# Refilling an expert weight ring in smaller fetches, copying gathered tokens earlier, and turning the activation in two halves

## What is computed

```python
def expert_block(args):
    xb, e = args
    hdn = xb @ w_up[e] + b_up[e]              # 1024 -> 2048
    x_glu = jnp.minimum(hdn[:, :D_FF], SWIGLU_LIMIT)
    x_lin = jnp.clip(hdn[:, D_FF:], -SWIGLU_LIMIT, SWIGLU_LIMIT)
    act = x_glu * jax.nn.sigmoid(SWIGLU_ALPHA * x_glu) * (x_lin + 1.0)
    return act @ w_down[e] + b_down[e]        # 1024 -> 1024
...
h = h + merged @ w_out[l]
h = h + moe_ffn(rms_norm(h, norm_ffn_g[l]), w_router[l], b_router[l], w_up[l], b_up[l], w_down[l], b_down[l])
h = rms_norm(h, norm_final_g)
```

## Time and profile before

| | us |
|---|---|
| median of 3 runs | 1189.77 |
| the profiled execution | 1189.58 |
| its span, first to last instruction | 1187.70 |
| PE busy | 1142.3 (96%) |
| mean granted TensorE clock, share of full speed | 0.997 |
| up of expert 0 starts at | 284.84 |
| up of expert 2 starts at | 344.17 |
| up of expert 4 starts at | 399.71 |

### The profile page before, as it was taken

How to read it: one execution, slowest core, us unless ns; L and a number is a source line. 1 busy time by engine, 2 the same in 40 slices (tenths; PEclk the granted TensorE clock), 3 DMA queues, 4 the chain that set the end, 5 groups by cost and what they waited for, 6 DMA issues and landing times.

```text
span 1187.7 us, 13231 instructions
## 1 busy us (share of the span) xinstructions
PE 1142.3 (96%) x5598; PEld 529.4 (45%) x5598; DVE 229.6 (19%) x527; ACT 187.3 (16%) x376; POOL 0.2 (0%) x4
## 2 busy tenths in 40 slices
PE   9999999999999999999999999999999999999996
PEld 7767888844243333333333334343333333333332
DVE  4555620114111111111111111111211111111112
ACT  2257620012010111101010101010110101000103
POOL 0000000000000000000000000000000000000000
PEclk9999999999999999999999999999999999999999
DMA  9834434384999999999999999999999999999996
GB/s 376 342 145 178 149 118 162 144 350 177 411 427 429 434 426 435 430 434 429 436 428 435 429 431 433 430 433 430 435 429 436 428 435 429 433 431 430 427 428 263
DMA packets 25117, 441.97 MB, mean 372 GB/s; under 512 B 4033, under 2 KB 4545, under 8 KB 7297
## 3 DMA queue, kind: packets, MB, share of 16 engines
q1 hardware_dynamic: 22464, 439.19, 87.5%
q10 hardware_dynamic: 2624, 2.39, 0.6%
HBM read 440.52 MB, written 1.05 MB: 372 GB/s over the span
## 4 chain that ended last, share of the span: by engine, by line
PE 83%; DMA 13%; ACT 2%; issue 1%; DVE 1%; ACTq 0%; SPq 0%; another core or an unknown queue 0%
PE ps L867 32%; PE ps L886 16%; DMA work<-in_w_exp_dram 12%; PE ps L525 11%; PE ps L842 4%; PE ps L854 4%; PE ps L734 2%; PE ps L797 2%; PE ps L817 2%; ACT work L1277 1%; PE ps L876 1%; PE ps L758 1%; PE ps L602 1%; DVE work L1720 1%; DMA ring<-in_w_mix_dram 1%
## 5 line engine op out<-in xcount | busy, mean ns | idle before, releaser
L867 PE MATMUL ps<-ring,work 128*64 128x512 f32 x1536 | 341.7, 597 | 5.6 <-DMA ring<-in_w_exp_dram 3.7
L867 PEld LDWEIGHTS ps<-ring,work 128*64 128x64 f32 x1536 | 108.5, 137 | 222.9 <-issue 216.6
L1719 DVE TENSOR_SCALAR work<-ps 128x512 f32<-128x512 f32 x32 | 22.1, 691 | 718.5 <-PE ps L867 718.5
L525 PE MATMUL ps<-work,ring 128*128 128x256 f32 (+2 forms) x576 | 129.6, 384 | 0.0
L886 PE MATMUL ps<-work 128*64 128x512 f32 x512 | 113.8, 595 | 10.6 <-ACT work L1277 10.3
L886 PE MATMUL ps<-ring,work 128*64 128x512 f32 x512 | 113.6, 595 | 8.4 <-ACT work L1277 7.0
L867 PE MATMUL ps<-work 128*64 128x512 f32 x512 | 116.0, 596 | 0.5 <-DMA work<-in_w_exp_dram 0.5
L525 PEld LDWEIGHTS ps<-work,ring 128*128 128x128 f32 (+1 forms) x576 | 107.1, 188 | 19.1 <-issue 1.2
L854 PE MATMUL ps<-work 64*128 64x512 f32 x256 | 71.7, 639 | 0.0
L886 PEld LDWEIGHTS ps<-work 128*64 128x64 f32 x512 | 35.2, 137 | 79.2 <-issue 62.8
L886 PEld LDWEIGHTS ps<-ring,work 128*64 128x64 f32 x512 | 35.5, 137 | 76.3 <-issue 65.1
(11 more groups left out here) (234 smaller groups left out, 620.8 us busy)
## 6 DMA issues: line engine op xcount, KB each, us to landing
ring<-in_w_exp_dram SPq DMA_DIRECT2D x56, 4096.0 KB, 33.6
work<-in_w_exp_dram SPq DMA_DIRECT2D x28, 4096.0 KB, 32.9
ring<-in_w_exp_dram SPq DMA_DIRECT2D x16, 2048.0 KB, 24.8
ring<-in_w_mix_dram SPq DMA_DIRECT2D x29, 1024.0 KB, 7.3
work<-in_w_exp_dram SPq DMA_DIRECT2D x6, 2048.0 KB, 20.0
work<-in_w_exp_dram SPq DMA_DIRECT2D x4, 1024.0 KB, 43.3
ring<-in_w_mix_dram SPq DMA_DIRECT2D x2, 576.0 KB, 17.8
work<-in_x_dram SPq DMA_DIRECT2D x2, 512.0 KB, 17.8
```

What stands on the lines that cost most here:

```text
L525: ins = nc.tensor.matmul(ps[part:part + width, b, 0:hi - lo], wv[:, k, o:o + width], xnT[:, k, lo:hi], start=(k == 0), stop=(k == KT - 1))
L867: ins = nc.tensor.matmul(ps[CAP * c:CAP * c + CAP, b, :], xeT[:, k, CAP * (u % 2):CAP * (u % 2) + CAP], wu[:, k % SPAN, 512 * q:512 * q + ...
L1719: V.tensor_scalar(hg, ps[:, 0, :], LIMIT, None, ALU.min).then_inc(glu_ready, 1)
```

## The change

There are four parts.

1. **Ring.** Experts 2 and 3 are fetched in units of 2 slots, and the very first unit in two halves of one slot each. `weights_used` now grows by one with every up step instead of by two with every second one. The loop over pairs starts with expert 4; the experts that no longer fill a group of four (28 and 29) are written out behind it.
2. **First copies.** ACT copies the first gather as soon as each half is done, ahead of the wait for `seed` and of its two DMAs.
3. **Turned activation.** `turn_act` puts the first two transposes into bank 3 and the other two into bank 2, each half with its own signal. ACT copies each half (256 columns) as it comes. `down` waits for the first half ahead of step 0 and for the second ahead of step 1. Since bank 2 also holds the turned routing weights, `turn_route` moves ahead of `up_bias`, both scatters are done first, and ACT copies the routing weights ahead of the activation.
4. **Root's table.** The dummy root that ACT runs to load the table of functions moves from ahead of the branch to behind it.

```diff
+            for h in range(SPAN):
+                spe.wait_ge(weights_used, M0 + h + 1)
+                spe.dma_start(RING[0][:, SLOT * h:SLOT * h + SLOT], w_exp[2, 0, :, SLOT * h:SLOT * h + SLOT])\
+                   .then_inc(unit_loaded[0], 16)
+            for n, c in [(2, c) for c in range(1, UNITS_E)] + [(3, c) for c in range(UNITS_E)]:
+                spe.wait_ge(weights_used, M0 + PER_EXPERT * (n - 2) + SPAN * (c + 1))
+                fetch(n, c)
...
-            with spe.Fori(0, (E - 4) // UNROLL) as it:
+            with spe.Fori(0, (E - 8) // UNROLL) as it:
                 for u in range(UNROLL):
                     for p in range(3):
-                        spe.wait_ge(weights_used, it * (UNROLL * PER_EXPERT) + (M0 + PER_EXPERT * u + 4 * (p + 1)))
...
+                        spe.wait_ge(weights_used, it * (UNROLL * PER_EXPERT) + (M0 + PER_EXPERT * (u + 2) + 4 * (p + 1)))
+                        fetch_pair(it, u, p)
...
-                    if k % SPAN == SPAN - 1:
-                        ins.then_inc(weights_used, SPAN)
+                    ins.then_inc(weights_used, 1)
...
             def turn_act():
-                for j in range(4):
-                    ins = nc.tensor.transpose(ps[:, 3, P * j:P * j + P], hl[:, P * j:P * j + P], ident)
-                return ins
+                for h in range(2):
+                    for j in range(2 * h, 2 * h + 2):
+                        ins = nc.tensor.transpose(ps[:, 3 - h, P * (j - 2 * h):P * (j - 2 * h) + P], hl[:, P * j:P * j + P], ident)
+                    ins.then_inc(actT_done, 1)
...
+            def down(n, unit_of):
                 for t in range(4):
+                    if t < 2:
+                        pe.wait_ge(actT_ready, n * 2 + (t + 1))
...
                 scatter(0, y, gpickT)
+                scatter(1, y, gpickT)
                 pe.wait_ge(route_ready, n + 1)
+                turn_route(2).then_inc(gpickT_done, 1)
                 pe.wait_ge(hidden_read, n + 1)
                 up_bias(1)
-                scatter(1, y, gpickT)
+                pe.wait_ge(gpickT_ready, n + 1)
                 pe.wait_ge(act_ready, n + 1)
-                turn_act().then_inc(actT_done, 1)
-                turn_route(2).then_inc(gpickT_done, 1)
-                pe.wait_ge(actT_ready, n + 1)
-                down(unit_of)
+                turn_act()
+                down(n, unit_of)
...
             act.wait_ge(pos_done, 2)
             nc.scalar.activation(counts, ps[:, 3, 0:E], ACT.Copy).then_inc(counts_read, 1)
+            for h in range(2):
+                act.wait_ge(gather_done, h + 1)
+                read_gather(h)
             act.wait_ge(seeded, 1)
...
-            for h in range(2):
-                act.wait_ge(gather_done, h + 1)
-                read_gather(h)
...
-            nc.scalar.activation(rs2[:, 0:1], rs2[:, 0:1], ACT.Sqrt)
...
+            nc.scalar.activation(rs2[:, 0:1], rs2[:, 0:1], ACT.Sqrt)
             for i in range(TT):
                 act.wait_ge(last_scat, i + 1)
```

More of the change, by code:

```diff
@@ L900, in unit_of @@
                     r = UNITS_E * (n % 2) + c
-                    pe.wait_ge(unit_loaded[r], 16 * landings)
+                    pe.wait_ge(unit_loaded[r], 16 * (landings + (n >= 2 and r == 0)))
                     return RING[r]
@@ L950, in odd @@
                 up_bias(0)
-                pe.wait_ge(xeT_ready, n + 2)
+                pe.wait_ge(xeT_ready, n + 3)
                 pe.wait_ge(act_ready, n + 1)
-                turn_act().then_inc(actT_done, 1)
-                pe.wait_ge(actT_ready, n + 1)
-                down(unit_of)
+                turn_act()
+                down(n, unit_of)
             seed(1, 0)
@@ L984, in _ @@
             pe.wait_ge(route_ready, 1)
+            turn_route(2).then_inc(gpickT_done, 1)
             pe.wait_ge(hidden_read, 1)
             up_bias(1)
+            pe.wait_ge(gpickT_ready, 1)
             pe.wait_ge(act_ready, 1)
[L988 to L991, removed]
+            turn_act()
+            down(0, alone(0, 1))
             odd(1, alone(1, 1))
-            with pe.Fori(0, (E - 4) // UNROLL) as it:
+            even(2, alone(2, 2))
+            odd(3, alone(3, 2))
+            with pe.Fori(0, (E - 8) // UNROLL) as it:
                 for u in range(UNROLL):
-                    n = it * UNROLL + (u + 2)
+                    n = it * UNROLL + (u + 4)
                     if u % 2 == 0:
@@ L1001, in _ @@
                         odd(n, paired(it, u))
+            even(E - 4, paired((E - 8) // UNROLL, 0))
+            odd(E - 3, paired((E - 8) // UNROLL, 1))
             pe.wait_ge(flag_ready, 1)
@@ L1010, in last_start @@
                     pe.wait_ge(xeT_ready, a + (k // 4 + 1))
-            up(0, alone(a, 2), last_start, lambda k: None)
+            up(0, alone(a, 3), last_start, lambda k: None)
             pe.wait_ge(y_ready, a + 1)
@@ L1073, in _ @@
                         pe.wait_ge(act_ready, n + 1)
-                        turn_act().then_inc(actT_done, 1)
-                        pe.wait_ge(actT_ready, n + 1)
+                        turn_act()
                         pe.wait_ge(gpickT_ready, n)
-                        down(again)
+                        down(n, again)
                         pe.wait_ge(y_ready, n + 1)
@@ L1274, in read_route, with read_act @@
                 return nc.scalar.activation(turned, ps[:, bank, 0:SEQ].rearrange("p (i t) -> p i t", i=TT), ACT.Copy)
-            def read_act(turned, bank):
-                return nc.scalar.activation(turned, ps[:, bank, :].rearrange("p (j t) -> p j t", j=4), ACT.Copy)
+            def read_act(n, turned, banks, o):
+                for h in range(2):
+                    act.wait_ge(actT_done, n * 2 + (h + 1))
+                    nc.scalar.activation(turned[:, 2 * h:2 * h + 2, :],
+                                         ps[:, banks[h], o[h]:o[h] + 256].rearrange("p (j t) -> p j t", j=2), ACT.Copy)                      .then_inc(actT_ready, 1)
             act.wait_ge(pos_done, 2)
             nc.scalar.activation(counts, ps[:, 3, 0:E], ACT.Copy).then_inc(counts_read, 1)
+            for h in range(2):
+                act.wait_ge(gather_done, h + 1)
+                read_gather(h)
             act.wait_ge(seeded, 1)
```

42 lines of the change are left out of this document (21 added, 21 removed).

## The result

The changed kernel takes **1183.10 us** (median of 5 runs, 1182.55 to 1183.32) against 1189.48 (median of 5, 1188.35 to 1191.97). The ratio is 0.9945, 95% interval 0.9932 to 0.9958, so it is 6.4 us faster, and the interval leaves out no change. The forecast was 1181.7 in a range of 1179.2 to 1185.6. The profiled execution took 1183.1 us, its span is 1181.2.

The account below looks back on a forecast made before the run. The prediction took the landing of the last weights as the bound. It summed 7.6 us from the earlier stream and 0.3 from the table, off the profiled 1189.58, to 1181.7 us, range 1179.2 to 1185.6.

Parts of the forecast that it names:

- The bound: Expert stage: the end is set by when the last weights land; TensorE time saved in the middle is worth nothing.
- Part 1: Weight stream: expert 4's first pair moves at 347.4 instead of 355.0, a term of 7.6 us.
- the ledger: Weight queue model: a fetch starts 0.95 us after issue or when the one ahead is through; a slot takes 2.43 us.
- the dry spots: Times the weight queue runs empty before expert 4: 3.2 us instead of 2.0, giving back some 1.3 us of 9.0.
- the fixed cost of the added fetches: Seven more weight DMAs at about 2.0 us each would cost 14 us; taken as zero, hidden behind the transfer ahead.
- Part 2: First gather's copies: `up` of expert 0 can start at 282.74, a gain of 2.10 us.
- The clock: TensorE at the first `up`: without the 1.94 us idle, no fall to 1.2 GHz is expected, saving 1.7 us.
- Part 3: Between up and down: 0.46 us less per expert, counted only as 2 x 0.46 before expert 4's first pair.
- Part 4: After the branch: the table load between first square and root goes; between 0 and 1.1 us, taken as 0.3.
- Slower: Rival: the clock falls in waits from expert 24 on and stays low over the last stretch, 1201 us; chance 0.05.
- The whole idle comes back: Rival: the queue is never dry at expert 4's first pair, so 9.0 + 0.3 us stays, 1180.3 us; chance 0.12.
- the ring's start is not what counts: Rival: a slower mixed stream or late later pairs spend the head start, gain under 2.4 us, 1188; chance 0.06.

Follow-up runs that it names:

- the two kernels with less data: Changed kernel with three of four slots fetched per pair for experts 4 to 29, then also with activation turned whole: 1159.82 and 1172.55 us.
- the ring alone: The kernel before with only the unit ring of part 1 added: median 1188.35 us, ratio 0.9981.
- the finest ring: Changed kernel with all units of expert 2 and expert 3's first down unit fetched slot by slot, experts 4 and 5 in units: 1183.63 us.
- with TensorE kept busy: The kernel before, with TensorE repeating another bank's seed twice while it would wait for the first gather's copies: 1188.81 us, ratio 0.9997.
- the whole turn: Changed kernel with the activation turned and copied whole again, new order kept: 1183.96 us.
- the kernel without early copies: Changed kernel with the first gather's copies again behind the wait for the seed and the two DMAs: median 1186.80 us.
- the one kept busy: The kernel without early copies, with TensorE also repeating another bank's seed twice during its wait: median 1185.66 us.

## Why the prediction was right, and where it was not

**The bound** was named rightly. The landing moved by 6.39 us and the time by 6.4, and the two kernels with less data show that TensorE's 12.7 us of savings appear only when the stream is not the limit.

**Part 1 and the sum.** Predicted: first bytes at 285.8, expert 4's first pair issued at 346.5 and moving at 347.45, a stream 7.6 us ahead. Measured: 285.6, 346.65, and by the ledger's own 0.95 us 347.6. The times of the events were right within 0.2 us. What was mis-sized is the term for **the dry spots**: of the 9.0 us won 1.3 were to be given back. The first bytes came 9.2 us earlier (285.62 against 294.82), and the lead was 7.2 us with 350 MB left and 6.5 with 2 MB left. So 2.0 us went in the first 27 MB, and 0.7 more in the long stretch behind them, to which the ledger gave nothing. The ledger knows only a queue that stands or runs at its full rate. The trace shows no standstill but thin stretches: 332 GB/s from 286 to 288, 299 from 296 to 300, 347 from 305 to 310, where the ledger has a stop of 2.3 us (the missing bytes are worth some 1.0 us, my estimate from the rate), and 328 to 344 from 348 to 352, behind a stop priced at 0.5 us. One or two fetches are in the queue there; that this is why it runs thin is argued, not shown. The other kernels agree: the ring was to be worth 2.8 to 2.9 us, and it gave 1.6 to 2.3 on top of parts 2 to 4. For the ring alone the runs do not tell 1.8 from 2.8.

The prediction took zero for the fixed cost of the added fetches, and nothing speaks against it: the finest ring has 12 more of them and took 1183.63, beside 1183.57 for the changed kernel. The section of the Trainium skill that it cites there (*DMA: Bandwidth & Descriptors*, Anatomy of one DMA) is about DMAs issued from GpSimd, and these go out on SyncE's queue, so the 14 us do not follow from it.

**Part 2.** `up` started at 282.70; 282.74 was predicted, and the 2.1 us are there. **The clock** was right for the two profiled executions (10.50 and 8.80 us for the same records), but I took it for a fixed cost. It is one of chance: it did not fall behind an idle of 2.78 us. The sum counts 1.7 us for it, and the profiled execution of the kernel before happened to have it. How much of it is in the 6.4 us of the medians is not shown: with TensorE kept busy, the median of the kernel before did not move clear of noise.

**Part 3.** 0.91 us from turned activation to down against 0.88 predicted, and no worth behind expert 2: right, by 1183.96 with the whole turn. TensorE began to wait for weights near 836 us, not 940: I compared it with the landing of each expert's first pair, but the second is the tighter one, since TensorE uses eight slots in 13.8 us and the stream brings them in 19.4. It costs nothing, since the landing decides.

**Part 4** was to give 0.3 and gives nothing that shows (17.17 us from landing to end with the load on either side, 17.26 in the kernel before). DVE's half of the output sets the first store, and I named DVE as late next without following it to the store.

**The rivals.** *Slower* rested on the clock falling in the waits for weights, which were to be 2.8 us and were 2.0. It did fall: four times, each for 3.4 us, in step with the stream. This window of the changed kernel is behind the wait that ended at 895.85:

```profile
898.00:900.00 2.00, 2.00 (x8) 0.86 (x6) 0.00 (x0) 0.00 (x0) 0.00 (x0) 0.50 0.95 410
```

And its timeline of TensorE around that wait:

```profile
886.94 7.04 PE L881 MATMUL ps<-ring,work 128*64 128x512 f32 x32
895.99 8.78 PE L881 MATMUL ps<-ring,work 128*64 128x512 f32 x32 [2.01 <-DMA ring<-in_w_exp_dram]
```

The 32 records behind the wait took 8.78 us, the 32 ahead of it 7.04. It came back each time and it cost nothing: the kernel without early copies had four such falls and the one kept busy had none, with four waits of 2.0 us in each, and both took 1185.66 in their profiled runs. The Trainium skill, page *TensorE: Matmul & The Clock Gate* (HAM oscillation), counts each fall behind a wait for data as lost time, in a case that computes for less time than it waits; here TensorE works some 56 us between two such waits, a fall does not follow each of them, and its price did not show, since data is the bound. *The whole idle comes back* and *the ring's start is not what counts* are out by the landings.

## What to carry to other kernels

When two engines both look full, ask which one's stock runs down. Here TensorE ate at 54 to 55 us what the queue delivered in 58, so the end was fixed by when the queue's unbroken stretch began. The same edit was worth 0.9 us there, and 12.7 us with a quarter of the data left out. To start a stream earlier pays only as far as every later release keeps up: find the first release that the queue waits for, and price the restart with more than its latency. A finer split went past that point with 1 to 2 us more of lead, and lost it again over the rest.

## What the runs showed that I had not expected

- The low clock behind a short idle is a matter of chance from one execution to the next: 1.94 and 2.51 us of idle ahead of the first `up` brought 3.4 us at 1.2 GHz, 2.78 us did not. The waits for weights in the twelve profiles with full data say it more broadly: of 34 waits of 2.00 to 2.05 us, 22 were followed by such a fall and 12 were not, four of four in one execution and none of four in another.
- The time from the last landing to the end was the same within 0.3 us (17.07 to 17.39) in twelve profiles. With such a constant, one row of the chain tells where an execution's time went. It does not tell why: the stream behind that row was up to 1.6 us further ahead than its landing.
- A stream that restarts with one or two fetches in its queue moved 328 to 344 GB/s over 4 us (348 to 352 in the changed kernel), against 432 when it is deep.
